# The u table turned by VectorE in 32 by 32 blocks, beside an attention loop with two sets of scores

## The chip, the cores and the metric

The kernel runs on one core of a Trainium2 chip. The metric is the device time of one execution in microseconds (us). The kernel before takes 3982.91 us, the median of three runs (3979.74 to 3983.61).

## What is computed

One layer of a diffusion backbone on 128 context tokens and 1024 latent tokens, width 1024, float32:

```
h = modulate(x, norm1_w, shift, scale);  z = h @ w_in
attention: 4 heads, q and k of 192 (128 + 64 rotary), v of 128, one softmax over 128 context and 1024 latent keys
retention: 4 heads, forwards and backwards, chunks of 128
x = x + g1 * (concat(att, ret) @ w_out);  h2 = modulate(x, norm2_w, ...)
PEER: scores against 2 x 128 sub-keys, 8 heads, top 16 of 16384 experts each
x = x + g2 * sum_k gate_k * gelu(u_table[e_k] . h2) * v_table[e_k]
```

`u_table` has 16384 rows of 1024. The kernel needs it in two layouts: with the width on the partitions, for the dense products, and row by row, for the tokens whose experts are gathered.

## The kernel before, in words

The work goes through stages, one after the other, each in a block with its own program for each engine: modulation, input projection (`stage_project`), q/k/v (`stage_qkv`), attention (`stage_attention`), retention, scores and top-k (`stage_scores`), experts (`stage_experts`). Between two stages all engines meet at a barrier. There are nine tiles of 128 tokens; tile 0 is the context.

The host hands the u table over as `uT[j][p][k][i]`: 128 blocks `j`, each with the 128 entries `p` of a slice `k` of the width on the partitions and 128 rows `i` in the free direction. The expert stage gathers whole rows of the table (L2261) from `u_rows`, which the kernel fills itself. So each block has to be turned: 8 transposes of 128 by 128, one for each slice `k`. That work shares no data with the stages beside which it runs. A block is 512 KB to load and 512 KB to store.

**Input projection.** The output columns are cut in nine chunks of 320. For each chunk TensorE goes through the nine tiles: 24 products (8 slices, high and low parts) into one of three PSUM banks (L636). ScalarE evicts each bank (L543 to L553) and issues the store of z from chunk 2 on (L555). GpSimd splits the weights of the next chunk in four parts (L509, L511). From chunk 1 on, after each of the tiles 0 to 7, TensorE turns one u block into PSUM (`turn_rows`, L644), VectorE copies it to one of two row buffers (`read_rows`, L613), and ScalarE's queue stores it (`store_rows`, L560). SP loads the blocks into four buffers (`load_keys`, L479), in one queue with the weights (`load`, L468). 8 chunks of 8 blocks make 64 of the 128 (`EARLY_ROWS`).

**Attention.** Tile by tile and head by head, 36 heads in all: four short ones with one block of keys (tile 0), and 32 whole ones with nine. For head n, TensorE makes the scores of head n+1 (L1084, L1085: two products for each cut of 512, 512 and 128 keys) into the one set of scores `ps_s`, transposes the nine blocks of probabilities of head n (L1109), and multiplies them with the values (L1118). VectorE takes the maxima (L1188), copies blocks 0 to 3 of the transposed probabilities (L1206), takes the reciprocal (L1207) and scales the result (L1211). ScalarE takes the exponential (L1144) and copies blocks 4 to 8 (L1154). GpSimd copies q of the head to a fixed place (L1066, L1067), since the loop over tiles runs on a register. From tile 1 on two u blocks belong to each head: TensorE turns each in two halves of four transposes (`turn_half`, L1096), the first half copied by VectorE (L1197), the second by ScalarE (L1163); SP loads (L1031) and stores (L1037) them. That makes the other 64 blocks. The order of the work is written out by hand on each engine; every step waits on a semaphore count.

Of the kernel before, what the change touches and what calls it, by code (L numbers as in the profile page):

```python
# [12 lines left out]
ALU = mybir.AluOpType  # L13
# [31 lines left out]
EARLY_ROWS = 64  # L45
# [376 lines left out]
def stage_project(nc, sem, m, keep, a):  # L422
# [15 lines left out]
    raws = [xt[0][:].rearrange("p (k c) -> p k c", k=KD), xt[1][:].rearrange("p (k c) -> p k c", k=KD),  # L438
            xn[:].rearrange("p (k c) -> p k c", k=KD), hT[:]]
    flat = keep.pairsT[:].rearrange("p r t -> p (r t)")  # L440
    rows = [flat[:, i * D:(i + 1) * D] for i in range(2)]
    u_in, row_out = [sem(f"rows_u_in{i}") for i in range(4)], [sem(f"row_out{i}") for i in range(2)]
    turned, rows_read = sem("rows_turned"), sem("rows_read")
    SHARE, SLOTS = TILES - 1, 2
# [8 lines left out]
    u_rows = keep.u_rows.rearrange("(j i) d -> j i d", i=P)  # L453
# [8 lines left out]
    with nc.Block() as block:  # L462

        @block.sync
        def _(sp):
# [10 lines left out]
            def load_keys(c, t):  # L476
                m = (c - 1) * SHARE + t
                sp.wait_ge(turned, m + 1)
                sp.dma_start(raws[t % 4], a["uT"][m]).then_inc(u_in[t % 4], 16)  # L479
# [4 lines left out]
            with sp.Fori(1, CHUNKS - 1) as c:  # L484
                for t in range(TILES - 1):
                    load_keys(c, t)
                    if t % 2:
                        load(c + 1, t // 2)
            for t in range(TILES - 1):
                load_keys(CHUNKS - 1, t)  # L490
            sp.wait_ge(ctx_in, 32)
            for i in range(SLOTS):
                sp.wait_ge(row_out[i], 16 * EARLY_ROWS // SLOTS)
# [22 lines left out]
        def _(act):  # L516
# [40 lines left out]
            def store_rows(c, t):  # L557
                m = (c - 1) * SHARE + t
                act.wait_ge(rows_read, m + 3)
                act.dma_start(u_rows[m], rows[t % SLOTS]).then_inc(row_out[t % SLOTS], 16)  # L560
# [13 lines left out]
            def late_chunk(c):  # L574
                for t in range(TILES):
                    evict(c, t)
                    if t:
                        store_rows(c, t - 1)
# [7 lines left out]
        def _(dve):  # L586
# [19 lines left out]
            dve.sem_inc(rows_read, SLOTS)  # L606

            def read_rows(c):
                for t in range(TILES - 1):
# [5 lines left out]
            read_rows(1)  # L615
            with dve.Fori(2, CHUNKS) as c:
                read_rows(c)

        @block.tensor
        def _(pe):  # L620
            pe.sem_inc(z_full, TILES)
            pe.sem_inc(turned, 4)
# [16 lines left out]
            def turn_rows(c, t):  # L639
                m = (c - 1) * SHARE + t  # L640
                pe.wait_ge(u_in[t % 4], ((c - 1) * (SHARE // 4) + (t // 4 + 1)) * 16)
                pe.wait_ge(rows_read, m + 1)
                for k in range(KD):
                    last = nc.tensor.transpose(pT[t % SLOTS][:, k, :], raws[t % 4][:, k, :], keep.ident)  # L644
                last.then_inc(turned, 1)
# [337 lines left out]
def stage_attention(nc, sem, m, keep, a):  # L983

    KT = TILES
    qcn = m.sb("qcn", [P, HEADS, P])
    qcr = m.sb("qcr", [P, 2, P])
    probs = [m.sb(f"probs{i}", [P, KT * P]) for i in range(2)]
    pT_sb = m.sb("pT_sb", [P, KT, P])
    sst = [m.sb(f"sst{i}", [P, 4]) for i in range(2)]  # L990
    ps_s = m.ps("ps_s", [P, 3 * 512])
    ps_t = m.ps("ps_t", [P, 12, P])
    ps_o = ps_t[:, 11, :]
    raws = [m.sb(f"key_cols{i}", [P, KD, P]) for i in range(4)]
    rows = [m.sb(f"key_rows{i}", [P, KD, P]) for i in range(2)]
    pU = m.ps("pU", [P, KD, P])
    HALF = KD // 2
    u_in, row_out = [sem(f"keys_in{i}") for i in range(4)], [sem(f"keys_out{i}") for i in range(2)]
    turned_a, turned_d, rows_a, rows_d = sem("keys_turned_act"), sem("keys_turned_dve"), sem("keys_rows_act"), sem("keys_rows_dve")
    u_rows = keep.u_rows.rearrange("(j i) d -> j i d", i=P)  # L1000
    SCALE = QK ** -0.5
    q_full, s_full, s_read, max_done, bias_done, p_full, t_full, pt_a, pt_d, o_full, rec_done, o_read = (
        sem(x) for x in ("q_full", "s_full", "s_read", "max_done", "bias_done", "p_full", "pt_full", "pt_act", "pt_dve",
                         "o_full", "rec_done", "o_read"))

    def spans(t):

        if isinstance(t, int) and t == 0:
            return [(0, P)], 1, 0
        return [(0, 512), (512, 1024), (1024, KT * P)], KT, 1  # L1010

    def has_rows(t):
        return not (isinstance(t, int) and t == 0)

    def row_block(t, h, x):

        return (t - 1) * 8 + (2 * h + x)

    with nc.Block() as block:

        @block.sync
        def _(sp):
# [5 lines left out]
            def load(t, h, x):  # L1028
                b, slot = row_block(t, h, x), h % 2 * 2 + x
                sp.wait_ge(turned_a, b + 1)  # L1030
                sp.dma_start(raws[slot][:], a["uT"][b + EARLY_ROWS]).then_inc(u_in[slot], 16)  # L1031

            def store(t, h, x):
                b = row_block(t, h, x)
                sp.wait_ge(rows_a, b + 2)
                sp.wait_ge(rows_d, b + 2)
                sp.dma_start(u_rows[b + EARLY_ROWS], rows[x][:].rearrange("p k c -> p (k c)")).then_inc(row_out[x], 16)  # L1037

            def four(t, part, stores=True):
                for h in (part * 2, part * 2 + 1):  # L1040
                    for x in range(2):
                        load(t, h, x)
                        if stores:
                            store(t - 1 + part, 2 - part * 2 + h % 2, x)

            four(1, 0, stores=False)
            four(1, 1)
            with sp.Fori(2, TILES) as t:
                four(t, 0)
                four(t, 1)  # L1050
            for h in (2, 3):
                for x in range(2):
                    store(TILES - 1, h, x)
            for x in range(2):
                sp.wait_ge(row_out[x], 16 * (N_KEYS - EARLY_ROWS) // 2 + 1)

        @block.gpsimd
        def _(pool):
            def copy(t):
                for h in range(HEADS):  # L1060
                    if not (isinstance(t, int) and t == 0):
                        pool.wait_ge(s_full, (t - 1) * HEADS + h + 1)
                    if h % 2 == 0:
                        if not (isinstance(t, int) and t == 0):
                            pool.wait_ge(s_full, (t - 1) * HEADS + h + 2)
                        nc.gpsimd.tensor_copy(qcr[:, h // 2, :], keep.qTr[:, h // 2, bass.ds(t * P, P)])  # L1066
                    nc.gpsimd.tensor_copy(qcn[:, h, :], keep.qTn[:, h, bass.ds(t * P, P)]).then_inc(q_full, 1)  # L1067

            copy(0)
            copy(1)  # L1070
            with pool.Fori(2, TILES) as t:
                copy(t)

        @block.tensor
        def _(pe):
            def scores(t, h):
                n = t * HEADS + h
                cuts, _, k0 = spans(t)
                pe.wait_ge(q_full, n + 1)
                if not (isinstance(n, int) and n == 0):  # L1080
                    pe.wait_ge(s_read, n)
                r = slice((h % 2) * ROPE, (h % 2 + 1) * ROPE)
                for lo, hi in cuts:
                    nc.tensor.matmul(ps_s[:, lo:hi], qcn[:, h, :], keep.kTn[:, h, k0 * P + lo:k0 * P + hi], start=True, stop=False)  # L1084
                    last = nc.tensor.matmul(ps_s[:, lo:hi], qcr[r, h // 2, :], keep.kTr[r, h // 2, k0 * P + lo:k0 * P + hi], start=False, stop=True)  # L1085
                last.then_inc(s_full, 1)

            def turn_half(t, h, x, q):
                if not has_rows(t):
                    return  # L1090
                b, slot = row_block(t, h, x), h % 2 * 2 + x
                if q == 0:
                    pe.wait_ge(u_in[slot], ((t - 1) * 2 + (h // 2 + 1)) * 16)
                pe.wait_ge((rows_d, rows_a)[q], b + 1)
                for k in range(q * HALF, (q + 1) * HALF):
# [1513 lines left out]
```

## Time and profile before

| | |
|---|---|
| median of the runs, us | 3982.91 |
| the profiled execution, us | 3974.01 |
| its span, us | 3972.2 |
| TensorE matmul / VectorE / ScalarE / GpSimd busy, share of the span | 92% / 76% / 32% / 43% |
| mean granted clock of TensorE | 0.952 |
| read from and written to HBM | 875 MB, 142 MB |

The span is what the records of the profiled execution cover; the execution's own time is 1.8 us more. Busy shares are means over stages with different limits. In the rows, L613 is line 613 of the kernel; "PE", "DVE", "ACT", "POOL", "SP" are TensorE, VectorE, ScalarE, GpSimd and SyncE, and a "q" behind an engine is its queue of transfers. The granted clock is a share of 2.4 GHz: 0.50 is 1.2 GHz. The input projection lies at about 106 to 465 us of the span, attention at 598 to 957 us.

### The profile page before, as it was taken

How to read it: one execution, taken by the hardware profiler on the slowest of the kernel's cores; microseconds unless marked ns; L12 is line 12 of the kernel's file. 1: busy time of each engine (PE TensorE's matmuls, PEld its weight loads, DVE VectorE, ACT ScalarE, POOL GpSimd, SP SyncE). 2: the span in 40 equal slices, each digit the busy share in tenths (PEclk: the TensorE clock that was granted, in tenths of full speed). 3: DMA queues.
4: the chain of work that ended last, by engine and by line, in shares of the span. 5: the costliest groups of instructions: out<-in, count | busy, mean ns of one | idle time of the engine just before them, and what ended most of it. 6: DMA issues, size and time to landing. Idle time of an engine off the chain costs nothing.

```text
span 3972.2 us, 58453 instructions
## 1 busy us (share of the span) xinstructions
PE 3664.3 (92%) x19218; PEld 3011.9 (76%) x19218; DVE 3026.1 (76%) x6011; ACT 1283.7 (32%) x1791; POOL 1693.7 (43%) x1065
## 2 busy tenths in 40 slices
PE   6999799998799993679999999999999999999998
PEld 2899765666654441468888888889988999999997
DVE  7322283334539998889999999989898988888888
ACT  6411152323312220753333333333232333233332
POOL 1222000002302332016555555556566777777774
PEclk9999897999999996569999999999999999999999
DMA  8588604666321010569999999999999999999997
GB/s 280 178 276 287 214 1 164 199 203 243 103 80 38 32 37 26 207 238 330 341 346 351 337 341 343 342 345 362 329 332 371 341 346 334 346 331 348 333 346 253
DMA packets 302496, 1018.14 MB, mean 256 GB/s; under 512 B 30583, under 2 KB 62107, under 8 KB 295099
## 3 DMA queue, kind: packets, MB, share of 16 engines
q1 hardware_dynamic: 153788, 484.39, 35.9%
q0 software_dynamic: 128880, 486.07, 33.5%
q10 hardware_dynamic: 19728, 46.61, 3.0%
q8 instruction: 33, 0.54, 0.1%
q14 instruction: 67, 0.54, 0.0%
HBM read 875.22 MB, written 141.72 MB: 256 GB/s over the span
## 4 chain that ended last, share of the span: by engine, by line
PE 35%; DVE 12%; DMA 6%; issue 6%; POOL 1%; ACT 0%; DVEq 0%; SPq 0%; ACTq 0%; POOLq 0%
PE p_y L2455 17%; PE p_a L2443 6%; PE p_a L2440 6%; PE p_a L2439 6%; DVE rows L2349 5%; DMA rows<-u_rows,pairsT 5%; DVE u_lo L2324 2%; DVE v_lo L2331 2%; DVE hot_w L2037 1%; POOL rows L2261 1%; DVE pairsT L2337 1%; DVE g_hi L2340 1%; DMA rows<-in_v,pairsT 1%; DVE hot_j L2033 0%; DVE h_rows L2362 0%
## 5 line engine op out<-in xcount | busy, mean ns | idle before, releaser
L2261 POOL DMA_INDIRECT rows<-in_v,pairsT x384 | 740.3, 1928 | 289.9 <-DVE h_rows L2362 195.4
L2261 POOL DMA_INDIRECT rows<-u_rows,pairsT x384 | 596.7, 1554 | 486.5 <-DVE pairsT L2349 415.0
L2439 PE MATMUL p_a<-h_hi,u_hi 128*128 128x384 f32 x2048 | 687.6, 336 | 4.1 <-DVE h_lo L2402 2.5
L2440 PE MATMUL p_a<-h_lo,u_hi 128*128 128x384 f32 x2048 | 691.1, 337 | 0.0
L2223 ACT ACTIVATE v_hi<-v_raw 128x1024 fp32r<-128x1024 f32 x256 | 272.0, 1062 | 748.0 <-PE p_y L2455 739.7
L2455 PE MATMUL p_y<-v_hi,g_hi 128*128 128x512 f32 x1536 | 488.8, 399 | 7.3 <-DVE g_hi L2340 6.9
L2349 DVE CUSTOM_DVE_ANT_0 rows<-rows,h_rows 128x1024 f32<-128x1024 f32 x384 | 451.4, 1220 | 53.5 <-DMA rows<-u_rows,pairsT 49.5
L2362 DVE SCALAR_TENSOR_TENSOR h_rows<-rows,pairsT,h_rows 128x1024 f32<-128x1024 f32 x381 | 467.7, 1279 | 16.7 <-DMA rows<-in_v,pairsT 16.7
L2455 PE MATMUL p_y<-v_lo,g_hi 128*128 128x512 f32 x1536 | 477.8, 392 | 0.0
L2443 PE MATMUL p_a<-h_hi,u_lo 128*128 128x384 f32 x2048 | 400.9, 337 | 18.9 <-DVE u_lo L2324 18.9
L2439 PEld LDWEIGHTS p_a<-h_hi,u_hi 128*128 128x128 f32 x2048 | 385.4, 188 | 15.2 <-issue 4.6
L2440 PEld LDWEIGHTS p_a<-h_lo,u_hi 128*128 128x128 f32 x2048 | 385.2, 188 | 9.8
L2455 PE MATMUL p_y<-v_hi,g_lo 128*128 128x512 f32 x1536 | 390.4, 389 | 0.0
L2443 PEld LDWEIGHTS p_a<-h_hi,u_lo 128*128 128x128 f32 x2048 | 360.2, 189 | 22.8 <-DVE u_lo L2324 22.7
L2455 PEld LDWEIGHTS p_y<-v_lo,g_hi 128*128 128x128 f32 x1536 | 289.4, 188 | 66.2
L2455 PEld LDWEIGHTS p_y<-v_hi,g_lo 128*128 128x128 f32 x1536 | 288.3, 188 | 59.9
L2455 PEld LDWEIGHTS p_y<-v_hi,g_hi 128*128 128x128 f32 x1536 | 279.7, 189 | 53.6 <-DVE g_hi L2340 9.2
L2324 DVE TENSOR_TENSOR u_lo<-u_raw,u_hi 128x1024 fp32r<-128x1024 f32 x256 | 311.6, 1218 | 5.1 <-ACT u_hi L2218 4.9
L2331 DVE TENSOR_TENSOR v_lo<-v_raw,v_hi 128x1024 fp32r<-128x1024 f32 x256 | 312.3, 1220 | 1.0 <-issue 1.0
L2054 ACT ACTIVATE wt<-pw 128x512 f32 (+1 forms) x144 | 156.2, 1085 | 403.4 <-PE pw L2046 395.1
L2218 ACT ACTIVATE u_hi<-u_raw 128x1024 fp32r<-128x1024 f32 x256 | 269.9, 1054 | 4.0 <-DMA u_raw<-in_uT 3.8
L613 DVE COPY pairsT<-pT 128x1024 f32<-128x1024 f32 x64 | 78.4, 1224 | 232.7 <-DMA u_rows<-pairsT 140.7
(335 smaller groups left out, 5849.3 us busy)
## 6 DMA issues: line engine op xcount, KB each, us to landing
u_raw<-in_uT SPq DMA_DIRECT2D x256, 512.0 KB
v_raw<-in_v SPq DMA_DIRECT2D x256, 512.0 KB
w_ring<-weights_spill POOLq DMA_DIRECT2D x32, 1536.0 KB
u_rows<-pairsT ACTq DMA_DIRECT2D x64, 512.0 KB, 5.8
key_cols<-in_uT SPq DMA_DIRECT2D x64, 512.0 KB, 4.1
u_rows<-key_rows SPq DMA_DIRECT2D x64, 512.0 KB, 4.7
wada<-in_w_ada SPq DMA_DIRECT2D x24, 1024.0 KB, 7.1
weights_spill<-wt SPq DMA_DIRECT2D x24, 1024.0 KB
```

Of the source, the lines that this page charges most:

```text
L2054: self.nc.scalar.activation(out.rearrange("p j b -> p b j"), banks[s % len(banks)], ACT.Copy, scale=1.0 / SHARE_UNIT).then_inc(self.pw_rea ...
L2218: nc.scalar.activation(u_hi[s][:], u_raw[s][:], ACT.Copy).then_inc(uhi_full, 1)
L2223: nc.scalar.activation(v_hi[s][:], v_raw[s][:], ACT.Copy).then_inc(vhi_full, 1)
L2261: pool.indirect_dma_start(rows[s][n % SLOTS][:], None, (keep.u_rows, v_rows)[g], at).then_inc(rows_in[s][n % SLOTS], 16)
L2324: nc.vector.tensor_sub(u_lo[s][:], u_raw[s][:], u_hi[s][:].bitcast(F32)).then_inc(ulo_full, 1)
L2331: nc.vector.tensor_sub(v_lo[s][:], v_raw[s][:], v_hi[s][:].bitcast(F32)).then_inc(vlo_full, 1)
L2349: nc.vector.tensor_tensor_reduce(out=slot[:], in0=slot[:], in1=keep.h_rows[:, s, :], op0=ALU.mult, op1=ALU.add, scale=1.0, scalar=0.0, acc ...
L2362: nc.vector.scalar_tensor_tensor(out=total, in0=slot[:], scalar=share, in1=total, op0=ALU.mult, op1=ALU.add).then_inc(rows_used, 1)
L2439: nc.tensor.matmul(p_a[:, 0:GT], u_hi[s][:, k, :], h_hi[:, k, :], start=k == 0, stop=False)
L2440: nc.tensor.matmul(p_a[:, 0:GT], u_hi[s][:, k, :], h_lo[:, k, :], start=False, stop=False)
L2443: last = nc.tensor.matmul(p_a[:, 0:GT], u_lo[s][:, k, :], h_hi[:, k, :], start=False, stop=k == KD - 1)
L2455: last = nc.tensor.matmul(p_y[i][:, half, :], part[s][:, i * P:(i + 1) * P], vv[s][:, half * 512:(half + 1) * 512], start=begin, stop=stop)
```

## The change

The turning of the u table goes from TensorE to VectorE, whose `transpose` turns the 32 by 32 blocks of a tile each for itself. For that, a transfer brings the table in another arrangement. A group of four blocks (512 rows) is cut in four pieces of two slices `k` each. In a piece, partition x holds four neighbouring entries `p` of the width (`e`) of one of the four blocks; after the turning it holds four neighbouring rows (`f`). The blocks of 32 by 32 are taken with a step of four elements, at the source (`(c f)`) and at the target (`(r e)`). Every contiguous run of a transfer is 1 KB, where it was 4 KB. A piece has 512 KB, as a block had; one VectorE instruction turns it.

48 pieces are turned in the projection: six for each of the chunks 1 to 8, through a ring of three source and three target buffers, the store issued after the evictions of tiles 1 to 6. The other 80 are turned in attention, through rings of five, two or three for each of the 36 heads.

Attention is written anew, without loops on registers: the scores of head n+2 are made while head n is finished, in one of two sets of scores; its PSUM banks for transposed probabilities are one for blocks 4 to 7 (`ps_mid`, copied by ScalarE) and one for blocks 0 to 3 (`ps_low`, copied by VectorE), and block 8 takes the place of block 0 once VectorE has copied it (`ps_last`, ScalarE). The result shares the bank of `ps_low`. GpSimd's copies of q are gone.

```diff
-EARLY_ROWS = 64
+EARLY_PIECES = 6
+PIECE = 2
 def stage_project(nc, sem, m, keep, a):
...
+    RING = EARLY_PIECES // 2
+    uT = a["uT"].rearrange("(m a) p k i -> m (a p) k i", a=4).rearrange("m (x e) k i -> m x e k i", e=4)
+    u_rows = keep.u_rows.rearrange("(m x f) (k d) -> m x f k d", x=P, f=4, k=KD)
...
             def store_rows(c, t):
-                m = (c - 1) * SHARE + t
-                act.wait_ge(rows_read, m + 3)
-                act.dma_start(u_rows[m], rows[t % SLOTS]).then_inc(row_out[t % SLOTS], 16)
+                act.wait_ge(turned, (c - 1) * EARLY_PIECES + (t + RING + 1))
+                act.dma_start(columns(u_rows, c, t), rows[t % RING]).then_inc(row_out[t % RING], 16)
...
-            def read_rows(c):
-                for t in range(TILES - 1):
-                    m, n = (c - 1) * SHARE + t, t % SLOTS
-                    dve.wait_ge(turned, m + 5)
-                    wait_count(dve, row_out[n], ((c - 1) * (SHARE // SLOTS) + t // SLOTS) * 16)
-                    nc.vector.tensor_copy(rows[n], pT[n][:].rearrange("p k c -> p (k c)")).then_inc(rows_read, 1)
+            def turn_rows(c):
+                for t in range(EARLY_PIECES):
+                    n, use = t % RING, (c - 1) * 2 + t // RING
+                    dve.wait_ge(u_in[n], use * 16 + 16)
+                    wait_count(dve, row_out[n], use * 16)
+                    turned_piece(nc, rows[n], raws[n]).then_inc(turned, 1)
...
                     multiply(c, s, t)
-                    if not first and t < TILES - 1:
-                        turn_rows(c, t)
 def stage_attention(nc, sem, m, keep, a):
...
+            for p in range(RING):
+                load(p)
+            for p in range(len(pieces)):
+                sp.wait_ge(turned, p + 1)
+                sp.dma_start(piece_of(u_rows, p), rows[p % RING][:]).then_inc(row_out[p % RING], 16)
+                if p + RING < len(pieces):
+                    load(p + RING)
...
+            for n in range(N):
                 pe.wait_ge(p_full, n + 1)
+                if whole(n):
+                    wait_count(pe, mid_kept, late(n) - 1)
+                    turn(ps_mid, n, 4, 8).then_inc(mid_full, 1)
+                wait_count(pe, o_read, n)
+                turn(ps_low, n, 0, min(4, blocks(n))).then_inc(low_full, 1)
+                scores(n + 2, FIRST)
+                if whole(n):
+                    pe.wait_ge(low_kept, n + 1)
+                    turn(ps_low, n, 8, 9).then_inc(last_full, 1)
+                scores(n + 2, REST)
+                values(n)
...
+            for n in range(N):
+                keep_turned(n)
+                exps(n + 2)
...
+            def turn_keys(p):
+                slot, use = p % RING, p // RING
+                dve.wait_ge(u_in[slot], use * 16 + 16)
+                wait_count(dve, row_out[slot], use * 16)
+                turned_piece(nc, rows[slot][:], raws[slot][:]).then_inc(turned, 1)
+
+            for n in range(2):
+                maxima(n)
+            for n in range(N):
+                keep_low(n)
+                maxima(n + 2)
+                inverse(n)
+                scaled(n)
+                for p in range(len(pieces) * n // N, len(pieces) * (n + 1) // N):
+                    turn_keys(p)
+
+def turned_piece(nc, rows, raw):
...
+    return nc.vector.transpose(rows.rearrange("p f k (r e) -> p e k f r", e=4), raw.rearrange("p e k (c f) -> p e k f c", f=4))
```

FIRST is the cut of the first 512 keys, REST the other two. `keep_low` waits for the values of head n-1 and for `low_full`, `scaled` for the values of head n. `keep_turned` is ScalarE's copy of blocks 4 to 7 and of block 8.

## Rows read from the trace of the kernel before

**Rows 1.** Table by stretches, us: engines' busy time (instructions), granted clock, transfers' share, GB/s

```profile
core 0: us, PE busy (x) PEld busy (x) DVE busy (x) ACT busy (x) POOL busy (x), PEclk, DMA share, GB/s
200.00:400.00 200.00, 200.00 (x1450) 199.77 (x1449) 50.20 (x41) 20.98 (x55) 45.72 (x40) 1.00 0.87 281
640.00:940.00 300.00, 289.53 (x1598) 187.24 (x1596) 113.27 (x203) 86.76 (x145) 10.02 (x39) 1.00 0.64 203
```

**Rows 2.** Waits from 163 to 470 us: us in total, times, longest

```profile
ACT z_rows L553 <- PE pz L636: 204.5, 53, 4.0
```

**Rows 3.** Timeline, ScalarE, projection: start us, us, instruction [idle before it]

```profile
155.27 0.44 ACT L543 ACTIVATE mix<-pz 128x320 f32<-128x320 f32 x1 [4.56 <-PE pz L636]
158.79 0.44 ACT L543 ACTIVATE mix<-pz 128x320 f32<-128x320 f32 x1 [3.08 <-PE pz L636]
163.18 0.44 ACT L543 ACTIVATE mix<-pz 128x320 f32<-128x320 f32 x1 [3.95 <-PE pz L636]
```

**Rows 4.** Timeline, VectorE, one head of attention

```profile
803.72 0.35 DVE L1211 TENSOR_SCALAR mix<-ps_t,sst 128x128 f32 x1 [1.50 <-PE ps_t L1118]
...
811.01 0.68 DVE L1206 COPY pT_sb<-ps_t 128x512 f32<-128x512 f32 x1
...
814.03 0.35 DVE L1211 TENSOR_SCALAR mix<-ps_t,sst 128x128 f32 x1 [1.50 <-PE ps_t L1118]
```

**Rows 5.** Timeline, TensorE, the same head

```profile
803.77 1.02 PE L1084 MATMUL ps_s<-kTn,qcn 128*128 128x512 f32 x2
...
805.78 1.12 PE L1084 MATMUL ps_s<-kTn,qcn 128*128 128x512 f32 x2
...
808.72 0.66 PE L1096 MATMUL pU<-grid,key_cols 128*128 128x128 f32 x4
809.21 1.15 PE L1109 MATMUL ps_t<-grid,probs 128*128 128x128 f32 x9
810.19 0.60 PE L1096 MATMUL pU<-grid,key_cols 128*128 128x128 f32 x4
...
811.64 2.17 PE L1118 MATMUL ps_t<-v_sb,pT_sb 128*128 128x128 f32 x18
813.65 0.60 PE L1096 MATMUL pU<-grid,key_cols 128*128 128x128 f32 x4
```

**Rows 6.** Groups by form, whole span: busy us, mean ns, idle before

```profile
L613 DVE COPY pairsT<-pT 128x1024 f32<-128x1024 f32 x64 | 78.4, 1224 | 232.7 <-DMA u_rows<-pairsT 140.7 <-PE pT L644 91.9
L1197 DVE COPY key_rows<-pU 128x512 f32<-128x512 f32 x64 | 44.2, 691 | 6.2 <-PE pU L1096 1.2 <-DMA u_rows<-key_rows 1.1
L602 DVE CAST h_hi<-hT 128x1024 fp32r<-128x1024 f32 x7 | 5.3, 751 | 14.7 <-ACT hT L534 14.7
...
L2054 ACT ACTIVATE wt<-pw 128x512 f32 x143 | 155.2, 1085 | 403.4 <-PE pw L2046 395.1 <-issue 8.3
L1163 ACT ACTIVATE key_rows<-pU 128x512 f32<-128x512 f32 x64 | 38.1, 595 | 48.9 <-PE pU L1096 48.9
```

**Rows 7.** Transfer queues from 1200 to 1300 us: packets, MB, share of 16 engines

```profile
q1 hardware_dynamic: 2656, 3.15, 9.5%
```

**Rows 8.** Timeline, first and last heads of attention, and the next stage's first operation

```profile
622.17 2.08 PE L1084 MATMUL ps_s<-kTn,qcn 128*128 128x512 f32 x2 [0.32 <-ACTq L1147]
...
631.64 1.12 PE L1096 MATMUL pU<-grid,key_cols 128*128 128x128 f32 x4
...
636.07 2.17 PE L1118 MATMUL ps_t<-v_sb,pT_sb 128*128 128x128 f32 x18
...
950.55 2.27 PE L1118 MATMUL ps_t<-v_sb,pT_sb 128*128 128x128 f32 x18
...
957.59 2.04 POOL L1336 TENSOR_TENSOR kb<-pairsT,dec 128x512 f32<-128x512 f32 x2 [54.94 <-POOLq L2502]
```

**Rows 9.** Table by stretches, columns as in rows 1: two stretches with a partly idle TensorE

```profile
1100.00:1110.00 10.00, 6.84 (x54) 6.08 (x53) 2.76 (x4) 1.92 (x4) 0.00 (x0) 1.00 0.53 174
1620.00:1740.00 120.00, 91.02 (x695) 68.29 (x695) 120.00 (x346) 93.41 (x89) 0.00 (x0) 0.50 0.48 199
```

More of the change, by code:

```diff
@@ L637, in multiply @@
                 last.then_inc(z_full, 1)
[L639 to L645, printed above, removed]
             def chunk(c, s):
@@ L1006, in spans @@
[L1006 to L1017, printed above, removed]
+    sst = [m.sb(f"sst{i}", [P, 4]) for i in range(HEADS)]
+    ps_s = [m.ps(f"ps_s{i}", [P, 3 * 512]) for i in range(2)]
+    ps_low, ps_mid = m.ps("ps_low", [P, 4, P]), m.ps("ps_mid", [P, 4, P])
@@ L1019, in stage_attention @@
+    o_full, rec_done, o_read = (sem(x) for x in ("o_full", "rec_done", "o_read"))
+    whole = lambda n: n >= HEADS
+    late = lambda n: max(n + 1 - HEADS, 0)
+    blocks = lambda n: KT if whole(n) else 1
+    first_key = lambda n: 1 if whole(n) else 0
     with nc.Block() as block:
@@ L1039, in four @@
[L1039 to L1072, printed above, removed]
+            def load(p):
+                sp.dma_start(raws[p % RING][:], piece_of(uT, p)).then_inc(u_in[p % RING], 16)
@@ L1074, in _ @@
+            for p in range(RING):
[5 more added lines that the diff above has]
+                    load(p + RING)
+            for x in range(RING):
+                sp.wait_ge(row_out[x], 16 * len(range(x, len(pieces), RING)))
         @block.tensor
         def _(pe):
[L1076 to L1082, printed above, removed]
-                for lo, hi in cuts:
-                    nc.tensor.matmul(ps_s[:, lo:hi], qcn[:, h, :], keep.kTn[:, h, k0 * P + lo:k0 * P + hi], start=True, stop=False)
-                    last = nc.tensor.matmul(ps_s[:, lo:hi], qcr[r, h // 2, :], keep.kTr[r, h // 2, k0 * P + lo:k0 * P + hi], start=False, stop=True)
-                last.then_inc(s_full, 1)
@@ L1088, in turn_half @@
[L1088 to L1095, printed above, removed]
-                    last = nc.tensor.transpose(pU[:, k, :], raws[slot][:, k, :], keep.ident)
-                last.then_inc((turned_d, turned_a)[q], 1)
@@ new lines, in turn, with values @@
+            def turn(out, n, lo, hi):
+                for k in range(lo, hi):
+                    last = nc.tensor.transpose(out[:, k - lo, :], probs[n % 2][:, k * P:(k + 1) * P], keep.ident)
+                return last
+            def values(n):
+                t, h = n // HEADS, n % HEADS
+                pe.wait_ge(low_kept, n + 1)
+                order = [*range(blocks(n))]
+                if whole(n):
+                    pe.wait_ge(mid_kept, late(n))
+                    pe.wait_ge(last_kept, late(n))
+                for k in order:
+                    last = nc.tensor.matmul(ps_o, pT_sb[:, k, :], keep.v_sb[:, first_key(n) + k, h * P:(h + 1) * P], start=k == 0, stop=k == order[-1])
+                last.then_inc(o_full, 1)
@@ L1165, in tile @@
[L1165 to L1180 removed]
+                if n >= 2:
+                    act.wait_ge(low_full, n - 1)
+                    wait_count(act, last_full, late(n - 2))
```

238 lines of the change are left out of this document (85 added, 153 removed).

## The prediction

> **What bounds the kernel now.** The profile's chain of work lies mostly in the expert stage, which the change doesn't touch, so I went to the table by stretches for the two stages it does touch [rows 1]. From 200 to 400 us (input projection) TensorE is busy for the whole stretch at the full clock, VectorE for a quarter of it, and the transfers for 0.87 of it at 281 GB/s. From 640 to 940 us (attention) TensorE is busy 96.5%, VectorE 38%, ScalarE 29%, transfers 64%. Both stages look bound by TensorE. The wait list says so for the first: ScalarE's evictions waited 204.5 us for the products and for nothing of note besides [rows 2]. So I read both stages as timelines. In the projection the pitch of evictions is 3.52 us where no turning of a block lies between two tiles, and 4.39 us where one does [rows 3]. In attention a head's pitch is 10.32 us, read off two successive scalings [rows 4], and TensorE's rows of that head [rows 5] split it: scores 4.95 (803.77 to 808.72), first half of a u block 0.49, probabilities 0.98 (809.21 to 810.19), two halves and a wait 1.45 (to 811.64), values 2.01 (to 813.65), last half 0.44. The u blocks so take 2.38 us of it, a wait of some 0.4 within.
>
> **Projection.** Removed from TensorE: 64 turnings (8 chunks of 8), each 4.39 - 3.52 = 0.87 us, all on its path: -55.7 us. Removed from VectorE are 64 copies at 1.224 us [rows 6]; added are 48 turnings (8 chunks of 6) of 128x1024, priced below. Even at 2.3 us they take 13.8 us of a chunk of 9 x 3.52 = 31.7, so they hide. SP issues 6 loads a chunk for 8, ScalarE's queue 6 stores for 8. ScalarE now waits for the turned piece and not for a copy; with a ring of 3, piece p+3 is turned only after the store of p has landed, which leaves 10.6 us (3 tiles) for landing and turning; the pools of three banks cover two tiles more. Bytes of a chunk: before 8 x 1.05 + 1.31 (weights) + 1.47 (z) = 11.2 MB in 38.7 us, 290 GB/s; after, 9.1 MB in 31.7, 286 GB/s. The rate that is asked for stays, so TensorE stays the bound. The packets become 1 KB where they were 4 KB. A stretch whose packets are mostly of 512 B moved 3.15 MB in 9.5% of 16 engines for 100 us [rows 7], 20.7 GB/s for each engine, against 281/0.87/16 = 20.2 in the projection [rows 1]; so I give small packets no price.
>
> **The turning on VectorE** decides the rest, and no row has one. It is 1024 elements a partition, and both its source and its target step by four floats (16 bytes) inside a block. Lower end: copies of the same size from SBUF go at 0.751 us on average [rows 6]. Next: 1.224 us, a plain copy from PSUM; two sizes (0.691 for 512) give 1.04 ns an element and 0.16 us fixed. The one strided write of this size class is ScalarE's at L2054, whose target steps by 16 floats: 1.085 us for 512 elements, where the unstrided copy at L1163 takes 0.595 [rows 6], so each element costs about twice. Doubling VectorE's 1.04 ns gives 0.16 + 2.13 = 2.29 us. I take 2.29, since the steps are what sets this instruction apart from a copy. Upper end: if read and write each add their own cost, 0.16 + 3.2 = 3.36 us.
>
> The Trainium skill speaks against the change here (Advanced Engine Details and Errata, section Memory Cachelines): SBUF is read and written in lines of 16 bytes, and an access that goes to another line each time pays a penalty. By that rule the instruction is a slow one, as by the row of L2054; by the rule alone no figure comes out.
>
> **Attention.** Work of TensorE for a head falls to 4.95 + 0.98 + 2.01 = 7.94 us. But VectorE's order now holds a chain: scale head n, turn 80/36 = 2.22 pieces, then copy the low four blocks of head n+1, for which TensorE waits ahead of its ninth transpose, the rest of the scores and the values. Round that loop: product to scaling 0.39 (813.65 less the period, 803.33, to 803.72), scaling 0.35 [rows 4], turnings 2.22 x 2.29 = 5.09, copy 0.68 [rows 4], handover and one transpose 0.2, rest of the scores 2.94 (805.78 to 808.72), values 2.01 [rows 5]: 11.66 us against 10.32. TensorE then idles some 3.7 us a head in front of the low copy. Over the 29 heads from the fifth of the whole ones on: +39 us. POOL's copies of q go, and with them a wait that cost nothing in the steady state; two sets of scores take the softmax off the path, which the chain above already assumes. SP carries 80 loads and stores for 64; 84 MB against 67 in a longer stage, no more GB/s than now; a ring of 5 gives each transfer two heads.
>
> Start: TensorE is at 1.2 GHz (granted clock 0.50), scores of a head last 9.5 us (622.17 to 631.6), and head 4 ends its values at 638.1 [rows 8]. The first four, short heads now carry two turnings each. The scores of heads 4 and 5 cover those of the later two; those of the first two, 9 us, lie open, and the first piece must land: +10 us. End: heads 34 and 35 have no scores to run: 11.66 - 2.94 = 8.7 each, against 10.3 and 5.0 now: +2. Behind the last values come 0.39 + 0.35 + three turnings 6.9 + from the last store to the next stage 3.7 = 11.3, against 5.0 now (952.6 to 957.6 [rows 8]): +6. Attention: +57 us.
>
> **Sum:** -55.7 + 57 = +1 us on the profiled 3974.0 us (its span is 3972.2, 1.8 lies around it), which lay 8.9 under the median of the three runs. On the median: 3984 us. The projection's gain is given back in attention.
>
> **Rivals.** First, the turning runs at the rate of a plain copy, 1.22 us: no stride cost. The loop is then 9.28 us, -1.04 x 29 = -30; start +5, last two heads -3, tail +3: attention -25, in all -81, 3902 us. For it: VectorE's large unstrided operations all take 1.22 us, and the row that doubles is another engine's, at a step of 64 bytes and not 16. The skill stands on this side too (Vector Engine (DVE) Microarchitecture Reference, section The reshape front-end and per-opcode configuration): a transpose sustains one element a cycle and lane. By that the time would be this rival's.
>
> Second, slower: the clock. TensorE now stands still for 3.7 us on average in each head, 6 us where three pieces fall to one head, and has no u transposes to fill. If the clock stays at its lower level through attention, the loop is 0.39 + 0.35 + 5.09 + 0.68 + 0.3 + 5.5 + 4.0 = 16.3 us (scores and values at twice their time): +6 x 29 = +174, less 56, plus the 18 of start and end: 4120 us. For it: from 1620 to 1740 us the clock was 0.50 with TensorE busy 76%. Against: from 1100 to 1110 it was 1.00 at 68% busy [rows 9]. It decides once more than one head in ten runs at the lower level.
>
> Third, the turning takes 3.36 us: loop 14.0, +108 in the steady part, +75 in all after the projection: about 4060. Fourth, 1 KB packets cost twice: the projection is bound by transfers, its gain turns into some +60 us, attention is too: over 4100.
>
> **How the numbers follow.** Forecast 0.52, own range 3965 to 4012 (a turning of 2.15 to 2.6 us, start 5 to 15). No stride cost 0.28; clock 0.08; 3.36 us 0.06; packets 0.06. A measurement can tell about 0.2%, 8 us, from no change. Faster: 0.28 + 0.05 of the forecast's lower end; same: 0.24; slower: 0.23 of the forecast's upper part + 0.20. The range leaves out the clock, the packets and the edges: 3895 to 4065.
>
> **What would show it.** The form of the turning in the table of groups: 2.29 or 1.22 us. Evictions 3.52 apart in the projection, at a full clock. A head's pitch of 11.7 us; TensorE idle before the ninth transpose, released by VectorE's low copy. Wrong if the pitch is under 10, if the clock is below 1.00 after 650 us, or if evictions in the projection wait for stores.

## The result, and the profile after

The changed kernel takes 4005.1 us (median of 6 runs, 3996.4 to 4023.0) against 3980.1 us (6 runs, 3974.7 to 3983.6): ratio 1.0067, interval 1.0045 to 1.009. It is slower by 0.7%. Its profiled execution took 4001.4 us with a span of 3999.6 us, 27.4 us more than before.

The table by stretches, with the columns of [rows 1]:

```profile
200.00:400.00 200.00, 200.00 (x1366) 200.00 (x1365) 78.79 (x38) 24.86 (x61) 45.28 (x40) 1.00 0.84 273
640.00:940.00 300.00, 243.55 (x926) 142.87 (x925) 161.70 (x171) 50.56 (x96) 0.00 (x0) 0.83 0.59 187
```

ScalarE's timeline in the projection, evictions of the products:

```profile
305.01 0.44 ACT L559 ACTIVATE z_rows<-pz 128x320 f32<-128x320 f32 x1 [3.16 <-PE pz L640]
308.46 0.44 ACT L559 ACTIVATE z_rows<-pz 128x320 f32<-128x320 f32 x1 [3.00 <-PE pz L640]
311.98 0.44 ACT L559 ACTIVATE z_rows<-pz 128x320 f32<-128x320 f32 x1 [3.08 <-PE pz L640]
```

TensorE is busy throughout and at the full clock, and the evictions lie 3.5 us apart, without the 4.39 of [rows 3]. Attention begins at 539.0 us and not at 597.9: 59 us are won ahead of it, 56.0 of them between the projection's evictions at 155.3 and 464.7 us before and the same two after (153.6 and 407.0). The second line of the table has the loss: in attention the mean clock fell from 1.00 to 0.83. TensorE is busy for 243.6 us of 300 where it was for 289.5, in part because the turnings are gone from it, in part because it waits.

The turning itself, in the groups by form (busy us, mean ns, idle before); the rows of before are the copies in [rows 6]:

```profile
L1160 DVE STREAM_TRANSPOSE key_rows<-key_cols 128x1024 f32<-128x1024 f32 x80 | 156.4, 2020 | 3.4 <-DMA key_cols<-in_uT 3.3
L1160 DVE STREAM_TRANSPOSE pairsT<-xt 128x1024 f32<-128x1024 f32 x32 | 66.3, 2076 | 125.6 <-DMA u_rows<-pairsT 121.0 <-DMA xt<-in_uT 4.6
```

One turning takes two microseconds, and two back to back take 3.87 to 4.00 us, 1.9 to 2.0 each. A head of attention with two turnings, at the full clock: VectorE's timeline (compare [rows 4]):

```profile
843.10 0.35 DVE L1137 TENSOR_SCALAR mix<-ps_low,sst 128x128 f32<-128x128 f32 x1 [0.66 <-PE ps_low L1064]
843.36 3.97 DVE L1160 STREAM_TRANSPOSE key_rows<-key_cols 128x1024 f32<-128x1024 f32 x2
847.17 0.71 DVE L1127 COPY pT_sb<-ps_low 128x512 f32<-128x512 f32 x1
...
853.33 0.35 DVE L1137 TENSOR_SCALAR mix<-ps_low,sst 128x128 f32<-128x128 f32 x1 [0.66 <-PE ps_low L1064]
```

TensorE's timeline of the same head (compare [rows 5]):

```profile
847.93 0.33 PE L1053 MATMUL ps_low<-grid,probs 128*128 128x128 f32 x1 [1.86 <-DVE pT_sb L1127]
848.10 1.02 PE L1046 MATMUL ps_s<-kTn,qTn 128*128 128x512 f32 x2
```

This is the loop that the prediction drew, product, scaling, turnings, low copy, ninth transpose, rest of the scores, values, at a pitch of 10.23 us. TensorE stands still for 1.86 us in the middle of the scores. And this is a head behind which three turnings fell (TensorE, 140 us earlier):

```profile
701.43 1.12 PE L1047 MATMUL ps_s<-kTr,qTr 64*128 64x512 f32 x2
706.24 0.33 PE L1053 MATMUL ps_low<-grid,probs 128*128 128x128 f32 x1 [3.69 <-DVE pT_sb L1127]
706.41 1.28 PE L1046 MATMUL ps_s<-kTn,qTn 128*128 128x512 f32 x2
707.62 2.07 PE L1047 MATMUL ps_s<-kTr,qTr 64*128 64x512 f32 x2
709.61 0.79 PE L1046 MATMUL ps_s<-kTn,qTn 128*128 128x128 f32 x2
```

The wait is twice as long, 3.69 us, and behind it two matmuls of 512 columns that took 1.12 us before it take 2.07: the clock has gone to its lower level (1.2 of 2.4 GHz) right behind the wait. It comes back during the values, and is lost again in the next head's scores, although the wait there is only 1.8 us. Three stretches of 20 us:

```profile
680.00:700.00 20.00, 16.16 (x78) 9.01 (x75) 12.27 (x15) 3.74 (x8) 0.00 (x0) 1.00 0.67 209
700.00:720.00 20.00, 14.42 (x49) 7.97 (x50) 12.50 (x11) 2.94 (x8) 0.00 (x0) 0.83 0.58 185
720.00:740.00 20.00, 18.10 (x60) 11.02 (x59) 7.90 (x10) 3.49 (x6) 0.00 (x0) 0.69 0.57 184
```

Note the last: TensorE looks busier (18.1 us) than in the first (16.2), and issues fewer instructions (60 for 78). Busy time at half the clock is half the work; the clock column has to be read beside it.

Heads are counted from 0, so the whole ones are 4 to 35. From head 5 to head 33 there are 29 waits ahead of the ninth transpose. The seven behind three turnings last 3.7 us, and in all seven heads the clock fell. The other 22 last 1.5 to 2.0 us; the clock fell in ten of these heads and stayed at 1.00 in twelve. So 17 of 29 heads were slowed. A slowed head lengthens two pitches, as its values end late too: of the 29 pitches from the values of one head to those of the next (heads 4 to 33), 23 exceed what the same turnings cost at the full clock, 12.1 to 13.1 us with two turnings (10.2 at the full clock) and 13.9 to 16.9 with three. For three turnings at the full clock there is no such pitch here; 12.1 is an estimate, 10.2 and 1.9 for the third turning.

The last marks: the first and the last two whole heads' values, and the next stage's first operation, as in [rows 8].

```profile
584.50 2.27 PE L1064 MATMUL ps_low<-v_sb,pT_sb 128*128 128x128 f32 x18
...
960.87 4.18 PE L1064 MATMUL ps_low<-v_sb,pT_sb 128*128 128x128 f32 x18 [0.46 <-ACT pT_sb L1104]
970.83 4.18 PE L1064 MATMUL ps_low<-v_sb,pT_sb 128*128 128x128 f32 x18 [0.46 <-ACT pT_sb L1104]
...
985.37 2.04 POOL L1268 TENSOR_TENSOR kb<-pairsT,dec 128x512 f32<-128x512 f32 x2 [630.01 <-POOLq L2434]
```

So attention takes 446.4 us (359.7 before), and what follows it takes nearly the same in both: 3014.2 and 3014.6 us. The whole difference lies ahead of attention and in it: -58.9 and +86.7.

### The profile page after: what moved, and what is told of

Read it like the earlier page. It is cut to its first block, busy times and chain, and to the rows that moved or that the text cites. A ratio compares the mean times of both kernels' runs of the same rounds, so it can differ in the third digit from the quotient of the medians.

```text
span 3999.6 us, 55222 instructions
## 1 busy us (share of the span) xinstructions
PE 3622.6 (91%) x18194; PEld 2950.0 (74%) x18194; DVE 3156.8 (79%) x6011; ACT 1255.4 (31%) x1759; POOL 1683.1 (42%) x1011
## 4 chain that ended last, share of the span: by engine, by line
PE 36%; DVE 12%; issue 5%; DMA 5%; POOL 1%; ACT 0%; DVEq 0%; SPq 0%; ACTq 0%; POOLq 0%
PE p_y L2387 18%; PE p_a L2375 6%; PE p_a L2372 6%; PE p_a L2371 6%; DVE rows L2281 5%; DMA rows<-u_rows,pairsT 4%; DVE u_lo L2256 2%; DVE v_lo L2263 2%; POOL rows L2193 1%; DVE hot_w L1969 1%; DVE pairsT L2269 1%; DVE g_hi L2272 1%; DMA rows<-in_v,pairsT 0%; DVE hot_j L1965 0%; DVE h_rows L2294 0%
```

## The experiments

Theory after the result: the turnings lie in a loop with the low copy; that makes TensorE wait inside the scores, and the wait of three turnings makes the clock fall. Rivals: the uneven dealing is harmless; the cost is the instruction's; the clock falls from something else (the scores themselves, VectorE's or the transfers' load).

**Turnings dealt evenly.** Four to each of the four short heads, two to each whole head:

```diff
+    first_piece = lambda n: 4 * n if n <= HEADS else 2 * n + 2 * HEADS
...
-                for p in range(len(pieces) * n // N, len(pieces) * (n + 1) // N):
+                for p in range(first_piece(n), first_piece(n + 1)):
                     turn_keys(p)
```

> The changed kernel with the same 80 turnings of attention dealt out evenly: four to each of the four short heads, two to each of the 32 whole ones, so that no whole head has three. Theory (the clock): in the changed kernel a head with three turnings leaves TensorE idle 3.7 us in one stretch, the granted clock falls behind it, and this and not VectorE's work is what the attention stage loses. Then the clock is 1.00 from the first whole heads on, the pitch of a head is 10.2 us throughout, attention falls from 446 us to about 390, and the kernel is 50 to 60 us faster than the changed one, 3940 to 3955 us. Rival (too little work): the clock falls because TensorE is busy only 80% of the time without the u transposes, however the turnings are dealt out. Then the clock stays at 0.7 to 0.85 in attention and the time stays within 15 us of the changed kernel's.

Measured: 3959.7 us, ratio to before 0.9955 (0.9938 to 0.9972). So the same work, dealt otherwise, turns the change from slower into slightly faster: 45 us under the changed kernel, a little less than the 50 to 60 expected. From 621 to 855 us every pitch is 10.18 to 10.22 us. Then, two stretches of the table:

```profile
840.00:860.00 20.00, 16.18 (x78) 9.42 (x78) 12.27 (x15) 4.16 (x8) 0.00 (x0) 1.00 0.66 210
860.00:880.00 20.00, 15.96 (x46) 8.24 (x44) 8.84 (x10) 2.46 (x5) 0.00 (x0) 0.72 0.52 158
```

And TensorE's timeline behind the wait in that second stretch:

```profile
862.52 0.48 PE L1054 MATMUL ps_low<-grid,probs 128*128 128x128 f32 x1 [1.82 <-DVE pT_sb L1128]
862.79 1.92 PE L1047 MATMUL ps_s<-kTn,qTn 128*128 128x512 f32 x2
```

The 24 heads before this one had the same wait of 1.8 us and kept their clock; this one lost it. So the expected "1.00 from the first whole heads on" was not met: three of the 29 waits of 1.8 us were followed by a fall. Three turnings are not needed for a fall; they bring one more often (seven of seven in the changed kernel). The five pitches above 10.2 from the first whole head on cost 12.7 us here, against 59 in the changed kernel. The rival of this run, that the clock falls because TensorE is busy only 80% of the time, can't be the whole cause: these 24 heads ran at 81% and 1.00.

**The low copy first.** VectorE copies the low blocks, then turns, then takes the maxima and scales:

```diff
                 keep_low(n)
+                for p in range(len(pieces) * n // N, len(pieces) * (n + 1) // N):
+                    turn_keys(p)
                 maxima(n + 2)
                 inverse(n)
                 scaled(n)
-                for p in range(len(pieces) * n // N, len(pieces) * (n + 1) // N):
-                    turn_keys(p)
```

> The changed kernel with VectorE's order within a head altered: low copy, then the two or three turnings, then maxima, reciprocal, scaling. It takes the turnings out of the loop from the scaling of one head to the low copy of the next. Theory (the loop): a head then costs about TensorE's own 7.9 us and small waits, 8.1 to 8.6 us, with a clock of 1.00; attention takes 310 to 335 us, the kernel 3865 to 3890 us. Rival (transfers or the clock): 84 MB in 300 us is 280 GB/s in pieces of 1 KB runs, and VectorE waits for loads or for the landing of stores, or TensorE's clock still falls; then the pitch stays at 9.3 us or more and the kernel above 3915 us.

Measured: 3883.2 us (3874.4 to 3887.7), ratio 0.9759 (0.9738 to 0.9779): some 95 us under the kernel before, 122 under the changed one, from two lines moved ahead of three others. Attention takes 318 us. VectorE's timeline of a head, and TensorE's ninth transpose in it, which no longer has a wait before it:

```profile
731.24 0.35 DVE L1137 TENSOR_SCALAR mix<-ps_low,sst 128x128 f32<-128x128 f32 x1 [0.66 <-PE ps_low L1064]
732.41 0.69 DVE L1127 COPY pT_sb<-ps_low 128x512 f32<-128x512 f32 x1 [0.82 <-PE ps_low L1053]
733.02 3.94 DVE L1160 STREAM_TRANSPOSE key_rows<-key_cols 128x1024 f32<-128x1024 f32 x2
...
734.15 0.33 PE L1053 MATMUL ps_low<-grid,probs 128*128 128x128 f32 x1
```

And the table by stretches, for most of the whole heads:

```profile
600.00:840.00 240.00, 232.26 (x1101) 133.01 (x1102) 194.18 (x204) 58.15 (x112) 0.00 (x0) 1.00 0.86 274
```

The turnings run while TensorE does the scores, the wait ahead of the ninth transpose is gone, pitches are 8.30 us (9.15 in the head behind three turnings) and the clock is 1.00. VectorE is now busy 81% and the transfers 86% of the time, at 274 GB/s, so neither load is what lowers the clock.

**Turning in unit steps.** What does the instruction itself cost? Only the access patterns change, so rows of u come out in another order (the experts read other rows; the time is what is looked at):

```diff
-    return nc.vector.transpose(rows.rearrange("p f k (r e) -> p e k f r", e=4), raw.rearrange("p e k (c f) -> p e k f c", f=4))
+    return nc.vector.transpose(rows.rearrange("p f k (e r) -> p e k f r", e=4), raw.rearrange("p e k (f c) -> p e k f c", f=4))
```

> The changed kernel with the turning instruction on neighbouring elements, at the source and at the target; loads and stores are as they were, so the rows of the u table land in other places than they should. Theory (the steps of 16 bytes): the instruction of 128x1024 falls from 2.02 to 2.08 us to 1.22 to 1.3 us; attention's loop for two turnings falls by 1.5 us to 8.7, three turnings leave 1.4 us less than now, and the kernel gains 60 to 90 us over the changed one. Rival (the transpose itself): a turning of float32 takes 2.0 us whatever its steps, and the time stays within 10 us of the changed kernel's.

Measured, groups by form:

```profile
L1160 DVE STREAM_TRANSPOSE key_rows<-key_cols 128x1024 f32<-128x1024 f32 x80 | 94.1, 1218 | 3.9 <-DMA key_cols<-in_uT 3.7
```

1.218 us: what the plain copy of this size took before (1.224 [rows 6]). So 0.80 of the 2.02 us are the steps of 16 bytes. One run took 3910.8 us, 94 under the changed kernel and more than the 60 to 90 expected; attention takes 349 us. The wait ahead of the ninth transpose shrinks to 0.5 us or less with two turnings, and the clock fell in none of these 22 heads. With three turnings it is 1.41 us, and the clock fell in five of seven:

```profile
764.99 0.33 PE L1053 MATMUL ps_low<-grid,probs 128*128 128x128 f32 x1 [1.41 <-DVE pT_sb L1127]
...
769.16 4.21 PE L1064 MATMUL ps_low<-v_sb,pT_sb 128*128 128x128 f32 x18
```

Two more kernels step on one side only, again with other rows' values in u.

> The turning reads neighbouring elements (columns dealt f c and not c f) and writes every fourth, so the rows of u hold other rows' values: a price alone. It took 2.02 us with both stepped and 1.22 us with neither. Theory (each side's step adds its share): about 1.6 us. Rival A (only the write pays, as ScalarE's strided write did): 2.02. Rival B (only the read pays): 1.22. Rival C (the slower side counts and both are alike): 2.02 here and with the other side stepped.

> The mirror of the kernel before it: the turning reads every fourth element and writes neighbouring ones (again other values in the rows of u). Theory (each side adds its share): about 1.6 us. Rival A (only the write pays): 1.22. Rival B (only the read pays): 2.02. Rival C (the slower side counts): 2.02.

Measured: 1.997 us with unit steps in the source alone, 1.984 us with unit steps in the target alone (80 each); one run each, 4002.9 and 4006.4 us. That is rival C of both: one stepped side costs as much as two, reading and writing at a step of 16 bytes cost the same, and mending one side brings no more than 0.04 us a turning.

**The new attention behind the old projection.** The projection of before (64 blocks turned on TensorE) with the changed attention, which so has 64 pieces for 36 heads, one or two each:

> The projection of the kernel before (TensorE turns 64 blocks) with the changed attention, which turns the other 64 blocks as 64 pieces: one or two for each head, never three. Theory (the clock falls behind three turnings only): clock 1.00 after the start, pitch 10.2 us with two turnings and 8.3 with one, mean 9.8; attention about 365 to 375 us against 360 before, the kernel 3975 to 3990 us. Rival (too little work on TensorE lowers the clock): clock under 0.9 and attention above 400 us, the kernel above 4010 us.

Measured: 4030.0 us in one run; attention 597.3 to 1010.5 us, 413 us against 360. The expectation that one and two turnings keep the clock failed, and the times are those of its rival, too little work on TensorE. TensorE, in a head behind two turnings that followed a head with one:

```profile
657.27 0.45 PE L1061 MATMUL ps_low<-grid,probs 128*128 128x128 f32 x1 [1.86 <-DVE pT_sb L1135]
657.51 1.92 PE L1054 MATMUL ps_s<-kTn,qTn 128*128 128x512 f32 x2
659.36 2.07 PE L1055 MATMUL ps_s<-kTr,qTr 64*128 64x512 f32 x2
```

A wait of 1.86 us, and the clock is gone, as in 15 of the 22 heads of this run that wait 1.4 to 2.0 us. The seven later heads behind one turning have no wait and none of them lost its clock. It is the heads with a wait that fall, and not the stage as a whole. The run also shows that the new attention by itself, with 64 pieces, loses 53 us.

**The wait filled.** If standing still is what lowers the clock, then work that is of no use should bring it back. TensorE makes 30 transposes of v into columns that nobody reads, ahead of its wait:

```diff
+                if whole(n) and n + 2 < N:
+                    for i in range(30):
+                        nc.tensor.transpose(ps_s[n % 2][:, KT * P:KT * P + P], keep.v_sb[:, 1 + i % 8, 0:P], keep.ident)
                 if whole(n):
                     pe.wait_ge(low_kept, n + 1)
```

> The changed kernel, and TensorE makes 30 transposes of v (into free columns of a bank of scores, read by nobody) between the first 512 columns of scores and its wait for the low copy: about 30 x 0.057 = 1.7 us, as long as the wait of a head with two turnings. VectorE's loop is as it was. Theory (the clock falls because TensorE stands still inside the scores; the turnings cost only what the loop costs at the full clock): granted clock 1.00 through the whole heads, pitch 10.2 with two turnings and 12.1 with three, so attention about 446 less 23 heads x 2.9 = 380 us, 3935 us in all. Rival (the clock falls by the scores themselves, or by VectorE's and the transfers' work): pitches of 13 to 16 stay, 4000 us or more.

Measured: 3981.8 us (3975.6 to 3985.1, 10 runs), ratio to before 1.0006 (0.9996 to 1.0016), some 23 us under the changed kernel. TensorE's timeline:

```profile
700.17 1.12 PE L1047 MATMUL ps_s<-kTr,qTr 64*128 64x512 f32 x2
701.23 3.50 PE L1080 MATMUL ps_s<-grid,v_sb 128*128 128x128 f32 x30
705.18 0.33 PE L1053 MATMUL ps_low<-grid,probs 128*128 128x128 f32 x1 [0.46 <-DVE pT_sb L1130]
705.34 1.02 PE L1046 MATMUL ps_s<-kTn,qTn 128*128 128x512 f32 x2
706.30 1.12 PE L1047 MATMUL ps_s<-kTr,qTr 64*128 64x512 f32 x2
```

The table by stretches:

```profile
640.00:900.00 260.00, 255.78 (x1525) 176.48 (x1526) 153.01 (x162) 46.24 (x90) 0.00 (x0) 1.00 0.63 199
```

The clock is 1.00 from 600 to 920 us, and no wait ahead of the ninth transpose is above 0.46 us there. Same scores, same turnings, same loads; the standing still is nearly gone. That rules out the rival. It doesn't tell one wait in a piece from the same idle time spread over the head, since the filling takes away both. The size was off: the transposes take 3.5 us and not 1.7, so the pitch with two turnings became 11.57 us instead of 10.2, and the time 3982 instead of 3935. The nine transposes of 128x128 in [rows 5], 0.98 us, would have given 3.3. A kernel with 105 us of useless TensorE work (30 heads of 3.5) is 23 us faster than the one without.

**Low copy first, dealt evenly.**

> The low copy ahead of the turnings, and the turnings dealt four to each short head and two to each whole head. With the low copy first, three turnings made the next head's pitch 9.15 and not 8.30, in about a quarter of the heads. Theory (those 0.85 us are the only cost left of uneven dealing): about 7 x 0.85 = 6 us less in the whole heads, up to 10 more at the start where the first transfers have to land for four turnings a head: 3875 to 3890 us, within 0.2% of the 3883 of the low copy alone. Rival (the clock still falls where three fall together): nothing to gain there, since it did not.

Measured: 3883.0 us (3878.9 to 3895.3), the same as with the low copy alone (3883.2). Once the turnings are off the loop, how they are dealt brings nothing here: whole heads hold 8.30 us, and the short heads, with four turnings each, give it back at the start (first whole head's values at 604.5 us, 593.5 with the plain dealing).

**The ninth block in a place of its own.** The other way to open the loop: TensorE needn't wait for VectorE inside the scores if the ninth block isn't turned into the first block's place. It now waits there for ScalarE's copy of that block, and the trace has no idle time for it.

```diff
-    ps_last, ps_o = ps_low[:, 0, :], ps_low[:, 3, :]
+    ps_last, ps_o = [x[:, 10 * P:11 * P] for x in ps_s], ps_low[:, 3, :]
...
                 turn(ps_low, n, 0, min(4, blocks(n))).then_inc(low_full, 1)
+                if whole(n):
+                    nc.tensor.transpose(ps_last[n % 2], probs[n % 2][:, 8 * P:9 * P], keep.ident).then_inc(last_full, 1)
                 scores(n + 2, FIRST)
-                if whole(n):
-                    pe.wait_ge(low_kept, n + 1)
-                    turn(ps_low, n, 8, 9).then_inc(last_full, 1)
+                wait_count(pe, last_kept, late(n))
                 scores(n + 2, REST)
...
-                    nc.scalar.activation(pT_sb[:, 8, :], ps_last, ACT.Copy).then_inc(last_kept, 1)
+                    nc.scalar.activation(pT_sb[:, 8, :], ps_last[n % 2], ACT.Copy).then_inc(last_kept, 1)
```

> The changed kernel with the ninth block turned into 128 free columns of a bank of scores instead of the place of the first block, so that it needn't wait for the low copy; VectorE's order (scale, turn the pieces, copy low) is unchanged. TensorE now runs both parts of the scores and waits for the low copy only ahead of the values, so the 2.67 us behind the ninth block leave VectorE's loop: 0.39 + 0.35 + 3.9 + 0.68 + 0.2 + 2.27 = 7.8 us with two turnings, less than the 8.3 us that TensorE needs for a head; 9.8 us with three. Theory (the wait inside the scores is the root of both the loop and the clock): pitch 8.3 and 9.8, granted clock 1.00 through the whole heads, attention about 330 us, 3885 to 3895 us. Rival (a wait anywhere in the head makes the clock fall, here 1.5 us ahead of the values after three turnings): pitches of 11 to 12 behind each head of three, 3910 or more.

> The ninth block in its own place and the low copy ahead of the turnings, both. With the low copy first nothing in TensorE's order waits for a turning except the low transposes of the next head, which want the scaling. Theory (each alone takes the turnings off the loop): no further gain, pitch 8.2 to 8.3, within 0.2% of the 3883 of the low copy first. Rival (the ninth transpose still waits some tenths for the low copy in that kernel): 0.3 us a head, 10 us less, 3873.

Measured: 3885.3 us (3878.0 to 3893.4), ratio 0.9768 (0.975 to 0.9787), and with both 3878.8 us (3871.6 to 3888.0), 0.9745 (0.9729 to 0.9762), the fastest median of all, though not apart from the other two. VectorE's order is that of the changed kernel in the first, so the order alone was not the fault: it was the order together with the wait inside the scores. Pitches are 8.34 us, and 9.13 with three turnings. The clock fell once in its heads 4 to 33, behind a head of three, where TensorE waits ahead of the values:

```profile
626.63 0.48 PE L1047 MATMUL ps_s<-kTr,qTr 64*128 64x128 f32 x2
627.83 3.70 PE L1064 MATMUL ps_low<-v_sb,pT_sb 128*128 128x128 f32 x18 [0.72 <-DVE pT_sb L1127]
```

The six other heads with such a wait (0.7 us, half of the 1.5 expected) kept the full clock.

## Why the prediction was right and wrong

The forecast was 3984 us, the kernel took 4005, inside its range of 3895 to 4065; its largest single chance, slower (0.43), came true. That is in part luck, as the terms show. One of its own signs of being wrong, a clock below 1.00 after 650 us, came too. From the profiled executions (negative is time won):

| term | predicted | measured |
|---|---|---|
| projection, to the start of attention | -55.7 | -58.9 (597.9 to 539.0) |
| start of attention, to head 4's values | +10 | +7.4 (45.5 for 38.1) |
| 29 whole heads, the loop at the full clock | +39 | +9.7 (309.1 for 299.4) |
| 29 whole heads, the clock | 0 | +59.2 (368.3 for 309.1) |
| last two heads | +2 | +2.9 |
| from the last values' start | +6 | +7.5 (14.5 for 7.0) |
| sum | +1 | +27.8 |

The 309.1 is an estimate: 22 pitches at 10.2 us and seven at 12.1. The values of the last two heads took 4.18 us for 2.17 and 2.27, so some 4 us of the last two lines are the clock's as well. Behind attention the changed kernel takes 0.4 us less, which gives the 27.4 between the spans.

**Right:** the projection, with no price for small packets. The transfers moved 273 GB/s at a share of 0.84 in the projection and 187 at 0.59 in attention, 20.3 and 19.8 GB/s for each of the 16 engines, and before, with runs of 4 KB, it was 20.2 and 19.8 ([rows 1]). The row that the prediction took for it was weak, though: 2048 of the packets of [rows 7] were of 512 B, but two thirds of the bytes went in 512 packets of 4 KB. The loads of 512 KB in runs of 1 KB did take longer from issue to landing in attention (6.7 us for key_cols, 4.1 before), but VectorE stood waiting for them for only 3.3 us in all. Right too was the loop, with every link of it and the place of TensorE's wait, and so were start and end. "It decides once more than one head in ten runs at the lower level" was the right thing to watch: 17 of 29 did.

**Mis-sized: the turning.** Predicted 2.29 us by doubling ScalarE's way, measured 2.02 to 2.08, and 1.9 to 2.0 back to back. With two turnings the loop's working gives 11.15 us and the trace 10.23: 0.77 of the difference is the turnings (3.81 us from the start of the two to the start of the copy), the rest is that scaling and turning overlap by 0.1 and the rest of the scores takes 2.84 and not 2.94. On average over two and three turnings it is 10.66 for 11.66. With this loop and no loss of clock the change would have been a gain of some 30 us. The third rival (3.36 us) fell with the same row, the first (no stride cost) with the 0.80 us that the unit steps saved. What the prediction said for the first, that VectorE's large unstrided operations "all take 1.22 us", doesn't hold of its own rows: the cast at L602 takes 0.751. The Trainium skill (Advanced Engine Details and Errata, section Memory Cachelines) has it that an access which goes to another 16-byte line each time pays; the three forms agree, and add its size here, 1.22 to 2.02 us, and that one such side is enough. The Trainium skill (Vector Engine (DVE) Microarchitecture Reference, section The reshape front-end and per-opcode configuration) has a transpose go at one element a cycle and lane. By the trace it went at the rate of a plain copy in unit steps alone (1.218 us for 1.224), and not at steps of 16 bytes.

**The step that failed: "+57 us" took the clock as 1.00 in the whole attention stage.** The prediction saw TensorE "stands still for 3.7 us on average in each head", and then treated the clock as a rival of all or nothing, at 0.08: either the whole stage at the lower level (4120) or none of it. What came is between: the clock went down behind a wait and came back with the values, in 17 of 29 heads, some 3.5 us for each, 59 us in all. The row that was held against it ([rows 9], 1.00 at 68% busy) was ten microseconds long and of another stage's work; it could not say what waits inside the scores would do. The filled wait shows that standing still is the cause: with no wait above 0.46 us the clock stayed at 1.00 through the heads up to 920 us. The Trainium skill (TensorE: Matmul & The Clock Gate, section HAM oscillation) says that an engine whose work comes in stretches between waits can be throttled again in each of them; the trace agrees for 17 heads of 29, and here the wait is for VectorE and not for a transfer.

So the sum was 27 us short mainly from two errors of opposite sign: the loop 29 too dear, the clock 59 left out. That they half cancel is luck: with the loop alone priced right the forecast would have been some 50 us too low.

**Open.** Why one head with a wait of 1.8 us loses its clock and the next with the same wait keeps it isn't settled. The length alone doesn't decide: all seven waits of 3.7 us from head 5 to 33 of the changed kernel were followed by a fall, but 28 of the 73 around 1.8 us (10 of 22 in the changed kernel, 3 of 29 with even dealing, 15 of 22 with 64 pieces), five of the seven of 1.41 us in unit steps, one of the seven of 0.7 us ahead of the values. Regular heads of 10.2 us kept it for 24 heads in a row. With 64 pieces every first wait behind a head that had none lost it (seven of seven); in the changed kernel the first short wait behind a long one did in three of seven. Nor is the kernel in unit steps shown as a usable one: its rows of u were in another order, and a form that puts them right by its transfers was not tried.

## What to carry to other kernels

When work is moved to an engine with time to spare, look for what that engine does next for the bounding engine, and put the moved work behind that, not ahead of it: here the turnings put behind the low copy turned 0.7% slower into 2.4% faster. Price a wait on TensorE twice, by its length and by the clock of the matmuls behind it (in the changed kernel a slowed head cost some 3.5 us on top of its wait), and read the clock column beside busy time. A wait in the middle of a run of matmuls can often be opened by giving one small result a place of its own.

## What the runs showed of the hardware that was not expected

- A wait of 1.8 us inside the scores could be enough for the granted clock to fall (from 1.02 to 1.92 us for two matmuls of 512 columns), in 28 of 73 cases, and a wait of 1.41 us in five of seven. Useless transposes in its place held the clock at 1.00 for 320 us.
- VectorE's 32 by 32 turning of 128x1024 f32: 1.218 us in unit steps, 1.98 to 2.00 us with one side at a step of 16 bytes, 2.02 with both. The costs of the two sides don't add.
- Thirty float32 transposes of 128x128 on TensorE took 3.5 us, 0.117 each, twice the 0.057 that the filler was sized by.
- SyncE's issue of one transfer of 512 KB in runs of 1 KB took 0.59 us for most stores and 0.64 to 0.74 for most loads in attention, 0.34 to 0.35 in runs of 4 KB.
